# The last expert load in two column halves, the last gate at the eviction, the residual in PSUM

## What is computed

```python
h2 = _rmsnorm(x, norm2_w[i]) * (1.0 + mod[:, 4]) + mod[:, 3]
x = x + mod[:, 5] * _expert_choice_ffn(h2, w_router[i], w_exp_gate[i], w_exp_up[i], w_exp_down[i])
...
return _rmsnorm(x, final_norm_w)
```

```python
gate, idx = lax.top_k(jnp.swapaxes(aff, 1, 2), cap)
xe = h[bidx, idx]
a = jnp.einsum('becd,edf->becf', xe, w_gate)
u = jnp.einsum('becd,edf->becf', xe, w_up)
ye = jnp.einsum('becf,efd->becd', jax.nn.silu(a) * u, w_down) * gate[..., None]
return jnp.zeros_like(h).at[bidx, idx].add(ye.astype(h.dtype))
```

## Time and profile before

| | us |
|---|---|
| median of 3 runs | 1383.29 |
| lowest and highest run | 1382.21, 1385.93 |
| span of the profiled execution | 1385.5 |
| TensorE busy in it | 1013.7 (73%) |
| VectorE, ScalarE, GpSimd busy | 529.2, 289.4, 28.7 |
| bytes moved | 415.13 MB |

### The profile page before, as it was taken

The page is one execution under the profiler, slowest core; times in us unless marked ns, Lnnn a source line. Parts: engine busy times, 40 slices in busy tenths (PEclk is TensorE's granted clock), DMA queues, the critical chain, the costliest instruction groups (busy, mean ns, idle before and its releaser), DMA issues.

```text
span 1385.5 us, 12873 instructions
## 1 busy us (share of the span) xinstructions
PE 1013.7 (73%) x5366; PEld 582.6 (42%) x5366; DVE 529.2 (38%) x983; ACT 289.4 (21%) x457; POOL 28.7 (2%) x42
## 2 busy tenths in 40 slices
PE   1797888799899997989887755555565656566574
PEld 0675767676576786677664211111111111011121
DVE  6976666775651697576754100000000000000002
ACT  3422343552331444542411000000000000000000
POOL 0000000100000001000010000000000000000000
PEclk9997889999999998899986978888867786767787
DMA  9895211577534576232376999999999999999994
GB/s 389 324 379 223 92 61 62 222 272 274 213 119 155 183 288 255 91 122 92 122 290 263 424 430 431 431 431 428 431 430 430 431 430 430 431 431 431 431 430 182
DMA packets 41001, 415.13 MB, mean 300 GB/s; under 512 B 4912, under 2 KB 4912, under 8 KB 7792
## 3 DMA queue, kind: packets, MB, share of 16 engines
q1 hardware_dynamic: 38160, 405.75, 71.8%
q10 hardware_dynamic: 2784, 8.57, 1.7%
HBM read 413.26 MB, written 1.05 MB: 299 GB/s over the span
## 4 chain that ended last, share of the span: by engine, by line
PE 41%; DMA 40%; DVE 13%; ACT 4%; issue 1%; POOL 1%; DVEq 0%; POOLq 0%; ACTq 0%
DMA ring<-in_w_egu 24%; DMA ring<-in_w_ed 12%; PE PS L633 7%; PE PS L634 7%; PE PS L635 7%; PE PS L934 3%; PE PS L1238 3%; DMA arena<-in_w_ed 2%; DVE ringR L1438 2%; PE PS L555 2%; PE PS L1300 2%; DMA ring<-in_w_in 1%; DVE arena L1315 1%; ACT ringR L2332 1%; PE PS L1288 1%
## 5 line engine op out<-in xcount | busy, mean ns | idle before, releaser
L1238 PE MATMUL PS<-ring,arena 128*32 128x512 f32 (+1 forms) x1152 | 174.8, 742 | 110.8 <-DMA ring<-in_w_egu 110.8
L633 PE MATMUL PS<-ringR,arenaR 128*128 128x512 f32 (+1 forms) x520 | 217.2, 418 | 31.6 <-DVE arenaR L1426 24.1
L634 PE MATMUL PS<-ringR,arenaR 128*128 128x512 f32 (+1 forms) x520 | 209.6, 403 | 0.0
L635 PE MATMUL PS<-ringR,arenaR 128*128 128x512 f32 (+1 forms) x520 | 209.1, 402 | 0.0
L1438 DVE TENSOR_TENSOR ringR<-ring,ringR 128x2048 fp32r<-128x2048 f32 (+1 forms) x66 | 148.7, 2254 | 105.5 <-ACT ringR L2332 100.5
L1315 DVE SCALAR_TENSOR_TENSOR arena<-arena,PS 128x256 f32<-128x256 f32 (+2 forms) x68 | 33.2, 498 | 373.9 <-ACT arena L2749 366.8
L2332 ACT ACTIVATE ringR<-ring 128x2048 fp32r<-128x2048 f32 (+1 forms) x66 | 123.9, 1884 | 88.0 <-PE PS L635 61.6
L1238 PEld LDWEIGHTS PS<-ring,arena 128*32 128x32 f32 x1152 | 36.5, 129 | 238.2 <-DMA ring<-in_w_egu 172.9
L1300 PE MATMUL PS<-ring,arena 128*32 128x512 f32 x512 | 86.4, 809 | 57.1 <-DMA ring<-in_w_ed 56.5
L633 PEld LDWEIGHTS PS<-ringR,arenaR 128*128 128x128 f32 x520 | 100.6, 194 | 59.0 <-DVE arenaR L1426 31.0
L555 PE MATMUL PS<-CT,arena 128*128 128x128 f32 (+1 forms) x352 | 65.3, 335 | 79.2 <-DVE arena L1315 27.6
(11 more groups left out here) (328 smaller groups left out, 865.5 us busy)
## 6 DMA issues: line engine op xcount, KB each, us to landing
ring<-in_w_egu SPq DMA_DIRECT2D x48, 2048.0 KB, 35.8
ring<-in_w_ed SPq DMA_DIRECT2D x32, 2048.0 KB, 34.6
ring<-in_w_vad SPq DMA_DIRECT2D x40, 1024.0 KB, 7.0
ring<-in_w_egu SPq DMA_DIRECT2D x24, 1536.0 KB, 30.0
arena<-in_w_egu SPq DMA_DIRECT2D x16, 2048.0 KB, 35.3
arena<-in_w_ed SPq DMA_DIRECT2D x12, 2048.0 KB, 32.6
ring<-in_w_in SPq DMA_DIRECT2D x22, 1024.0 KB, 4.8
ring<-in_w_gu SPq DMA_DIRECT2D x22, 1024.0 KB, 4.8
```

The costliest lines, as they stand in the source:

```text
L633: mm(o, xh(k, t), hi[:, c], start=k == 0, stop=False)
L634: mm(o, xh(k, t), s.viewr[:, c], start=False, stop=False)
L635: i = mm(o, xl(k, t), hi[:, c], start=False, stop=k == nk - 1)
L1238: i = mm(PS[32 * ee:32 * ee + 32, b + a_, 0:fw], XEv[:, k, grp, 32 * ee:32 * ee + 32], wv[:, ee, a_, :], start=k == 0, stop=k == 7, tile_p ...
```

## The change

- The last load (group 3, block 10, named by `LAST_ED`) becomes two loads of 1 MB, one for each half of the output columns, into slots 14 and 15, each with its own semaphore. For that the down weights lie in memory with the column half outside the expert, in all blocks.
- TensorE does the 4 matmuls of the first half when the first of these has landed, and those of the second when the second has.
- The gate row is multiplied in when the down results are evicted, in all four groups. VectorE does both halves; ScalarE's eviction goes.
- `X` is added by four matmuls of the identity with `X` that open the sums in banks 0 to 3, ahead of the twelve of L1288.
- The four scatter matmuls of group 3 have hh outermost.
- ScalarE squares and sums each half row from PSUM, four instructions of 512 columns in place of two of 1024. GpSimd adds the two sums and epsilon in one instruction (`rstd_of_two`). VectorE's last scaling reads PSUM. The two passes over each tile (gate, residual) go.

```diff
+LAST_ED = (3, NDOWN - 1)
...
-                want("ed", (grp, c), D["w_ed"][grp * NDOWN + c], MSLOT)
+                src = D["w_ed"][grp * NDOWN + c]
+                if (grp, c) == LAST_ED:
+                    for hh in range(2):
+                        want("ed", (grp, c, hh), src[:, SLOT * hh:SLOT * hh + SLOT], SLOT)
+                else:
+                    want("ed", (grp, c), src, MSLOT)
...
+            if k[0] == "ed" and k[1][0:2] == LAST_ED and len(k[1]) > 2:
+                s, m = (4, 6, 12, 14, 0, 2, 8, 10)[(turn["ed", (*LAST_ED, 0)] - first_moe) % 8] + k[1][2], 1
...
                 if grp == 3:
                     w.wait_ge(*at("v moe he", 11))
+                    for t in range(2):
+                        for hh in range(2):
+                            mm(PS[:, 2 * t + hh, :], ident, Xv[:, t, 512 * hh:512 * hh + 512], start=True, stop=False)
                     for g3 in range(3):
-                        w.wait_ge(*at("v moe ye", g3))
-                        w.wait_ge(*at("a moe ye", g3))
+                        w.wait_ge(*at("v moe ye", g3, 1))
                         for t in range(2):
                             for hh in range(2):
-                                mm(PS[:, 2 * t + hh, :], SGT[:, 256 * g3 + 128 * t:256 * g3 + 128 * t + 128],
-                                   YE[:, 1024 * g3 + 512 * hh:1024 * g3 + 512 * hh + 512], start=g3 == 0, stop=False)
+                                i = mm(PS[:, 2 * t + hh, :], SGT[:, 256 * g3 + 128 * t:256 * g3 + 128 * t + 128],
+                                       YE[:, 1024 * g3 + 512 * hh:1024 * g3 + 512 * hh + 512], start=False, stop=False)
+                    i.then_inc(*sig("pe moe x"))
...
+                    if (grp, c) == LAST_ED:
+                        for hh in range(2):
+                            s = slot("ed", (grp, c, hh))
+                            w.wait_ge(*s.ready)
+                            down(c, hh, s.view).then_inc(*sig("pe moe last", hh))
...
-            for t in range(2):
-                for hh in range(2):
-                    w.wait_ge(*(at("a moe ye", 3) if hh else at("v moe ye", 3)))
-                    i = mm(PS[:, 2 * t + hh, :], SGT[:, 768 + 128 * t:896 + 128 * t], YE[:, 3072 + 512 * hh:3584 + 512 * hh], start=False, stop=True)
-                i.then_inc(*sig("pe moe out", t))
+            for hh in range(2):
+                w.wait_ge(*at("v moe ye", 3, hh))
+                for t in range(2):
+                    mm(PS[:, 2 * t + hh, :], SGT[:, 768 + 128 * t:896 + 128 * t], YE[:, 3072 + 512 * hh:3584 + 512 * hh],
+                       start=False, stop=True).then_inc(*sig("pe moe out", t, hh))
...
-                w.wait_ge(*at("pe moe dn", grp, 10))
-                cp(YE[:, 1024 * grp:1024 * grp + 512], PS[:, 6, :]).then_inc(*sig("v moe ye", grp))
-            T = XE[:, 0:1024]
+                w.wait_ge(*at("a gate row", 3))
+                for hh in range(2):
+                    w.wait_ge(*(at("pe moe last", hh) if grp == 3 else at("pe moe dn", grp, 10)))
+                    tt(YE[:, 1024 * grp + 512 * hh:1024 * grp + 512 * hh + 512], PS[:, 6 + hh, :], mods2[:, 1024 + 512 * hh:1536 + 512 * hh],
+                       ALU.mult).then_inc(*sig("v moe ye", grp, hh))
+            w.wait_ge(*loaded("fin"))
+            w.wait_ge(*at("pe moe x"))
             for t in range(2):
-                w.wait_ge(*at("pe moe out", t))
-                chain()
-                w.wait_ge(*at("a gate row", 3))
-                tt(T, PSF[:, 1024 * t:1024 * t + 1024], mods2[:, 1024:2048], ALU.mult).then_inc(*sig("v fin"))
-                chain()
-                tt(Xv[:, t, :], Xv[:, t, :], T, ALU.add).then_inc(*sig("v fin x", t))
-            w.wait_ge(*loaded("fin"))
-            for t in range(2):
+                w.wait_ge(*at("pe moe out", t, 1))
                 w.wait_ge(*at("g fin rs", t))
-                stt(Xv[:, t, :], Xv[:, t, :], st4[:, 2 + t:3 + t], fn, ALU.mult, ALU.mult).then_inc(*sig("v fin out", t))
+                stt(Xv[:, t, :], PSF[:, 1024 * t:1024 * t + 1024], st4[:, 4 + t:5 + t], fn, ALU.mult, ALU.mult).then_inc(*sig("v fin out", t))
...
-                w.wait_ge(*at("pe moe dn", grp, 10))
-                act(YE[:, 1024 * grp + 512:1024 * grp + 1024], PS[:, 7, :], ACT.Copy).then_inc(*sig("a moe ye", grp))
-            for t in range(2):
-                w.wait_ge(*at("v fin x", t))
-                act(two(junkf)[:, t, :], Xv[:, t, :], ACT.Square, scale=1.0 / 32, accum_out=st4[:, t:t + 1]).then_inc(*sig("a fin sq", t))
+            for hh in range(2):
+                for t in range(2):
+                    w.wait_ge(*at("pe moe out", t, hh))
+                    act(two(junkf)[:, t, 512 * hh:512 * hh + 512], PS[:, 2 * t + hh, :], ACT.Square, scale=1.0 / 32, accum_out=st4[:, 2 * hh + t:2 * hh + t + 1]).then_inc(*sig("a fin sq", hh, t))
...
-                w.wait_ge(*at("a fin sq", t))
-                rstd("fin", t, dst=st4[:, 2 + t:3 + t], ms=st4[:, t:t + 1])
+                rstd_of_two("fin", t, st4[:, 4 + t:5 + t], st4[:, t:t + 1], st4[:, 2 + t:3 + t])
...
-    d["w_ed"] = np.ascontiguousarray(wd.reshape(4, 4, NDOWN, 128, 1024).transpose(0, 2, 3, 1, 4)).reshape(4 * NDOWN, 128, MSLOT)
+    d["w_ed"] = np.ascontiguousarray(wd.reshape(4, 4, NDOWN, 128, 2, 512).transpose(0, 2, 3, 4, 1, 5)).reshape(4 * NDOWN, 128, MSLOT)
```

More of the change, by code:

```diff
@@ L531, in used @@
             if name == "ed":
-                return at("pe moe dn", *i)
+                return at("pe moe dn", *i) if len(i) == 2 else at("pe moe last", i[2])
             return at(f"pe {name} slot", i)
@@ L1290, in tensor, with down @@
+                    i.then_inc(*sig("pe moe x"))
+                def down(c, hh, wv):
+                    for ee in range(4):
+                        i = mm(PS[32 * ee:32 * ee + 32, 6 + hh, :], HT[:, 128 * c + 32 * ee:128 * c + 32 * ee + 32], wv[:, 512 * ee:512 * ee + 512],
+                               start=c == 0, stop=c == 10, tile_position=(0, 32 * ee))
+                    return i
                 for c in range(NDOWN):
-                    s = slot("ed", (grp, c))
-                    w.wait_ge(*s.ready)
@@ L1293, in tensor @@
                     w.wait_ge(*at("a moe ht", n - 1))
                     if grp:
-                        w.wait_ge(*at("v moe ye", grp - 1))
-                        w.wait_ge(*at("a moe ye", grp - 1))
-                    for hh in range(2):
[L1298 to L1301, removed]
@@ L1302, in tensor @@
-                    i.then_inc(*sig("pe moe dn", grp, c))
-            for t in range(2):
-                for hh in range(2):
-                    w.wait_ge(*(at("a moe ye", 3) if hh else at("v moe ye", 3)))
-                    i = mm(PS[:, 2 * t + hh, :], SGT[:, 768 + 128 * t:896 + 128 * t], YE[:, 3072 + 512 * hh:3584 + 512 * hh], start=False, stop=True)
-                i.then_inc(*sig("pe moe out", t))
+                        w.wait_ge(*at("v moe ye", grp - 1, 1))
+                    if (grp, c) == LAST_ED:
[3 more added lines that the diff above has]
+                            down(c, hh, s.view).then_inc(*sig("pe moe last", hh))
+                    else:
+                        s = slot("ed", (grp, c))
+                        w.wait_ge(*s.ready)
+                        for hh in range(2):
+                            i = down(c, hh, s.view[:, 2048 * hh:2048 * hh + 2048])
+                        i.then_inc(*sig("pe moe dn", grp, c))
```

## The result

The change makes the kernel faster by about 5.4 us: the ratio to the kernel before is 0.9961, 95% interval 0.9951 to 0.9971, from 13 runs each, medians 1385.93 and 1380.87 us. Forecast was a saving of 4.9 us. The median of before rose from 1383.29 (3 runs) to 1385.93 with ten more runs, which shows how widely one program scatters (1382.2 to 1394.3); the ratio is the number to hold on to. A median run after takes 1380.87 us, which is 2.5 above the forecast of 1378.4, because the median of before stands 2.6 higher than the one that the forecast started from. The profiled execution after has a span of 1378.3 us, 7.2 less than the one of before. Not all of that belongs to the change.

A forecast was written before the change was run, and what follows sets the result against it. Bound: the weight stream until the last load lands, then 18.1 us of dependent work. Saving 5.6 us on the span, less 0.7 for the median, is 4.9: 1383.3 to 1378.4 us; range 1375.6 to 1381.4.

The forecast's parts named there:

- The bound and the landing: Last weight load: second half lands at 1367.4 us as before, first 2.44 us earlier; one more load costs 0.
- Rival 2: Last load: split brings less, by a 1.4 us price or both halves landing together; 1379.4 to 1379.8 us, chance 0.08.
- X in PSUM costs nothing: Last group: four identity matmuls take 3.9 us, covered by the load queue; without the cover they cost 3.9 us.
- The gate at the eviction: Down eviction: VectorE's gate product takes 691 ns against 692 for a copy; last group's first half done before second landing.
- TensorE behind the landing: After the last landing: 8 down records in 0.97 us, then scatter in 3.70 us, at full clock.
- rival 1: TensorE's clock falls in the tail: saving 4.0 us against the span, 1379.3 to 1380 us, chance 0.19.
- The prediction's own sign against it: Scatter after the last landing: a clock of 0.5 there would show the forecast wrong.
- GpSimd: Reciprocal root in the tail: two pairs of steps, 1.72 us for the first tile, 1.67 us for the second.
- rival 3: Reciprocal root: GpSimd is quick in both tiles, 1.2 us more saved, 1377.2 us, chance 0.10.
- The scaling and the stores: End of kernel: VectorE scales the second tile from 1375.6 to 1376.9 us, then output takes 3.0 us.
- Rival 4: Late issue of the last three loads passes fully to the landing: 1.8 us slower, 1385.1 us, chance 0.03.
- The 0.7 us taken off between span and median: Whole run: the median before holds half of the profiled last block's 1.45 us half-clock loss, so 0.7 us less saving.

The follow-up runs named there:

- the second set: The changed kernel run once more, unaltered, against the kernel before: ratio 0.998, tail 12.9 us.
- the two delayed ones: The changed kernel with 16 or 24 useless matmuls behind those that add X; landing waits (stream) 55.64 and 61.51 us, one run each.
- split_only: The kernel before with only the last load split by output columns; ratio to before 1.0008, tail 16.6 us.
- late24: The changed kernel with 24 useless matmuls behind those that add X; stream 61.51 us, tail 11.2 us, one run.
- keep_clock: The changed kernel with useless matmuls in TensorE's gaps before and between the last halves; ratio to before 0.9949, tail 11.2 us.
- beside_sbuf: The changed kernel with one useless VectorE product, operands outside PSUM, started with GpSimd's first pair; tail 14.0 us, one run.

## Why the prediction was right

The sign and the size came out (4.9 us forecast, 5.4 measured, 4.0 to 6.8 by the interval), and the tail too: 12.5 us forecast, 12.9 measured. But two of its terms were wrong by some 1.6 us each and cancelled, so that it came out this closely is luck. The saving itself is that of the first set; the second set has 2.8.

- **The bound and the landing.** Right. The stream was 55.07 us before and 55.15 after, and between 55.05 and 55.17 in every kernel but the two delayed ones. The halves came 2.48 us apart (2.44 forecast). One more load in the queue cost at most 0.09 us (split_only's stream). The Trainium skill's fixed 2.0 us per DMA ("DMA: Bandwidth & Descriptors", section "Anatomy of one DMA") is fitted to DMAs issued through GpSimd, which the prediction left out. These loads are issued by SP, and queued as they are, they show no such price: 0.09 us at most. Rival 2 is refuted with it.
- **X in PSUM costs nothing.** Right. The eight records took 4.85 us, four of them at a granted clock of 0.50, but those behind them took 10.46 instead of 11.64. The issues came 3.5 us later, where 3.9 was forecast, and the stream didn't notice; without the four matmuls it was no shorter. The cover was somewhat overestimated: a delay of 17.2 us cost 0.5, where I had about 20 covered.
- **The gate at the eviction.** Right: 0.69 us each, the first ahead of the last landing, the second under the scatter.
- **TensorE behind the landing.** Mis-sized. I took the full clock on the grounds of the shorter gaps, 4.7 us. Measured were 6.35 (rival 1 in its mechanism, though its saving was off by what follows). The prediction's own sign against it, a clock of 0.5 in the scatter, came: 0.50 for its first 1.6 us. The step that failed is the inference from the length of a gap: the gap ahead of the half block was 1.42 us, near the 1.35 of the earlier trace rows, and the clock was low all the same. The trace of before already spoke against it, with the full block behind 2.91 us shown above. (The "1.2 us left" at a low clock for the whole tail should read 0.9: 5.6 less 4.67.)
- **GpSimd.** Mis-sized, and the reason is shown. I took 1.72 and 1.67 us from the earlier trace rows; measured were 0.93 and 0.94. Neither was a property of the place: VectorE worked beside them on two operands outside PSUM, in the tail on the residual add, which the change removes. From the first pair's start to the end of the second it took 1.96 us, not 3.5. This was rival 3, at 0.10, though its time needed the full clock as well.
- **The scaling and the stores.** Since GpSimd was quick, VectorE's two scalings follow each other and end 1.6 us behind the second pair, not 1.3. The output's 3.06 us agree with the 3.0. That the stores were nearly the bound (4.2 us from the first issue) wasn't seen.

In sum 1.65 (clock) - 1.54 (GpSimd) + 0.29 (scaling) + 0.06 (output), less 0.04 by which GpSimd started before TensorE's end, is 0.42 us over the forecast tail of 12.5: the 12.9 measured. Rival 4, the delay passed on, is refuted at this size; of the 24.0 us of late24, 6.4 are passed on. The 0.7 us taken off between span and median was a guess, and no run tests it, since the kernel before wasn't profiled at full clock. Its ground was off, too: a run's time lies 1.9 us above its span (1380.25 and 1378.3 after), so the profiled execution of before, with a span of 1385.5, would be at about 1387.4, above all three runs and not near the slowest.

What stays open: why whole runs scatter by several us, beyond the one profile in which the clock in the attention shows it; why the times of split_only show no gain; and how much of the 1.7 us of keep_clock a median run gains, as the changed kernel may get the full clock by itself in some runs.

## What to carry to other kernels

At the end of a stream of loads, split the last one by what the tail consumes, not by what is loaded: the first half's compute and eviction then hide under the second half's transfer, worth 1.8 us here at full clock. No run splits the load in another way. When a step looks slow in a trace, look at what ran beside it before carrying its duration to a place where that neighbour is gone. And once a tail has been cut, count back from the last store: here the two stores set the end, 4.2 us behind the first issue, and an earlier scaling of the second tile alone brought 0.1 us.

## What the runs showed of the hardware

GpSimd's step on 128x1 numbers took 0.30 us beside VectorE reading PSUM, 1.33 beside a product of two operands outside it (beside_sbuf), and ended 0.1 us after that product. TensorE's useless matmuls in its gaps kept the granted clock at 1.00 where it had been 0.73, and the tail was 1.7 us shorter with more work. A further load in the full queue cost at most 0.09 us of stream (split_only). Two stores of 0.5 MB issued 0.65 us apart landed 2.6 and 3.2 us after their issue.
